# A hybrid two-block transformer on one core: in the recurrent stage the chunk inverse is kept as 64x64 blocks and turned on two quadrants, masked products alternate heads, one scan serves all chunks

## The chip, the cores and the metric

The kernel runs on one core of a Trainium2 chip. A core has TensorE (matmuls, PE in the rows; its weight loads are PEld), VectorE (DVE), ScalarE (ACT), GpSimd (POOL) and SyncE (SP, which issues the weight transfers). The metric is device time in microseconds for one launch, the median of several runs. Lower is better.

## The reference

Two transformer blocks with batch 1, 512 tokens and width 1024, in fp32. The first has sparse and latent attention and an MLP; the second, where the change lies, has an RWKV-7 mixer beside a convolution, a gated merge and an MLP. The mixer's recurrence, for each of 16 heads of 64 channels:

```
def _wkv7_scan(r, w, k, v, kk, a):
    """RWKV-7 recurrence. Inputs (B, T, H, N); state S (B, H, N_value, N_key).
    S_t = S_{t-1} diag(w_t) + (S_{t-1} (-kk_t)) (kk_t * a_t)^T + v_t k_t^T ;  o_t = S_t r_t
    """
    n_chunks = t // CHUNK
    ...
    _, o = lax.scan(chunk_step, S0, inputs)
```

CHUNK is 64, so there are 8 chunks. The kernel does not step through the tokens: within a chunk it builds a 64x64 triangular matrix from kk and a, inverts it by doubling blocks (5 levels), and then chains the 8 chunk states.

## The kernel before

The work is written out by hand, in one order for all engines. For the recurrent stage `rwkv_order()` yields a list of steps; each engine's program walks the same list and emits its own share of each step, with semaphores between the engines. An engine's instructions run strictly in this order. PSUM's banks are handed out in the list's order too (`begin` waits until the bank's former content has been emptied).

The stage is a loop over j = 0 to 7. A tile j is 128 channels, that is two heads (hh 0 and 1 on partitions 0 to 63 and 64 to 127); its 512 tokens stand as TT = 4 blocks t of 128, each two chunks. In quadrant form, the first chunk of a block is on rows 0 to 63, the second on rows 64 to 127 (`own_chunks`). A tile goes through these steps:

- `tok` turns four tiles to token-major form (L1139); `mb`, `mk` are the products of `arow` with `bh` and `kh` (L1147); VectorE masks them into `ma`, `mr`, `ka`, `kr` (L2142, L2144).
- `iy0` starts the inverse: head 0 on VectorE (L2132, L2133), head 1 on GpSimd (L738, L742). `ip` holds 64x64 blocks. `iy` (the inverse so far) and `ix` (its transpose) hold 128x128 per block t, of which only the chunks' own 64x64 blocks are read.
- `gnm`, `gnv`, `gnb`, `gnend`: the group norm of the tile before, put among these steps (L1239, L1243, L1125; VectorE L2189 and L2194 to L2204; ScalarE squares at L1625 and takes a root at L1628).
- for each level: `inv` turns `iy` on TensorE (L1156) and ScalarE copies it to `ix` (L1334); `ip` multiplies by `ma` (L1167) and VectorE masks it (L2153); `iy` multiplies (L1172) and VectorE adds (L2161).
- `akv`, `opv` (L1162, L1195), `tav` (L1178), `rr` (L1184), `opa` (L1202), `pt`, `qq`, then the chain of states `st` (L1226, L2182, L2185) and `ost` (L1234).

Between the steps stand parts of the next tile's projections (L765 to L767: three fp32r matmuls of 512 columns for each of 8 parts), its own first steps (`lw2`, `scan`, `kk`, ...), and on VectorE the 31 taps of the convolution (L2005). The weights of the projections are split into a high and a low half by ScalarE (L1295) and GpSimd (L680).

`scan` sums the log decays within each chunk: eight scans of 64 columns (L2071).

Of the kernel before, what the change touches and what calls it, by code (L numbers as in the profile page):

```python
# [24 lines left out]
P = 128  # L25
# [125 lines left out]
def rwkv_order():  # L151
# [3 lines left out]
    for j in range(KT):  # L155
# [16 lines left out]
        out += [("akv", j, 0), ("akv", j, 1), ("inv", j, 1, 0), ("opv", j, 0), ("opv", j, 1)]  # L172
# [10 lines left out]
        out += [("tav", j, 0), ("tav", j, 1)] + slot(1) + [("rr", j, 0), ("rr", j, 1)] + slot(1)  # L183
        out += [("opa", j, 0), ("opa", j, 1)] + last[:1] + [("pt", j, 0), ("pt", j, 1)] + last[1:2] + [("qq", j, 0), ("qq", j, 1)]
# [215 lines left out]
def rwkv_constants():  # L400
# [5 lines left out]
    out = [own(i < t), same & (i <= t)]  # L406
# [9 lines left out]
CONSTS = {"rw": (1 + LEVELS + 1 + 1) * CH + 2 * P, "eye_ones": 2 * P + H // 2, "alibi": S, "cmpb": TT * NC, "causal": S, "rope": S}  # L416


def build_program(nc, io):
    x_in, vec_in, w_in, out = io["x"], io["vec"], io["w"], io["out"]  # L420
    ctx = ExitStack()
    with ctx:
# [72 lines left out]
        with ExitStack() as at:  # L495
# [30 lines left out]
            ix, iy, ip = both("ix", TT * P), both("iy", TT * P), both("ip", TT * CH)  # L526
            iy2 = [m.rearrange("p t (c n) -> p t c n", c=2) for m in iy]
# [15 lines left out]
        strict, incl = rw[:, 0:CH], rw[:, CH:CH + P]  # L543
        level = [rw[:, CH * (3 + lv):CH * (4 + lv)] for lv in range(LEVELS + 1)]
        own_eye = rw[:, CH * (4 + LEVELS):CH * (5 + LEVELS)]
        heads = rw[:, CH * (5 + LEVELS):CH * (5 + LEVELS) + P]
# [125 lines left out]
        def _(pool):  # L672
# [22 lines left out]
            for f in rwkv_order():  # L695
# [28 lines left out]
                elif kind == "re":  # L724
                    wait_emptied(pool, ("rkv", j, 0))
                    pool.wait_ge(exp_ready, 2 * j + 2)
                    if j:
                        wait_filled(pool, ("mk", j - 1, 1))
                        wait_emptied(pool, ("rr", j - 1, 1))
                        wait_emptied(pool, ("rr", j - 1, 0))  # L730
# [3 lines left out]
                elif kind == "iy0" and f[2] == 1:  # L734
                    wait_emptied(pool, ("mb", j, 1))
                    if j:
# [5 lines left out]
                    pool.tensor_tensor(iy2[1], ip[1].unsqueeze(2).to_broadcast([P, TT, 2, CH]),  # L742
                                       own_eye.unsqueeze(1).unsqueeze(1).to_broadcast([P, TT, 2, CH]), ALU.add).then_inc(iy0_done[1], 1)
# [4 lines left out]
        def _(pe):  # L748
# [330 lines left out]
            for f in rwkv_order():  # L1079
# [69 lines left out]
                elif kind == "inv":  # L1149
# [5 lines left out]
                    for t in range(TT):  # L1155
                        mm = pe.transpose(b[:, t * P:t * P + P], iy[hh][:, t, :], eye)  # L1156
# [6 lines left out]
                elif kind == "ip":  # L1163
                    hh, lv = f[2], f[3]
                    wait_emptied(pe, ("inv", j, hh, lv - 1))
                    for t, own in own_chunks:
                        mm = pe.matmul(b[own, t * CH:t * CH + CH], ma[hh][own, t, :], ix[hh][own, t, own], start=True, stop=True)  # L1167
# [516 lines left out]
        def _(dve):  # L1684
# [330 lines left out]
            for f in rwkv_order():  # L2015
# [49 lines left out]
                elif kind == "scan":  # L2065
# [310 lines left out]
```

## Time and profile before

| | |
|---|---|
| median of 3 runs | 2250.59 us (2247.04 to 2252.44) |
| profiled execution | 2251.5 us, its span 2249.7 us |
| granted clock of TensorE, mean | 0.971 of 2.4 GHz |
| busy: TensorE, its weight loads | 2103.1 us, 1650.2 us |
| busy: VectorE, ScalarE, GpSimd | 1188.6 us, 800.9 us, 736.3 us |
| recurrent stage | about 1008 to 1648 us |

In a row of the profile, "L1184 PE MATMUL psum<-mr,tav 128*64 128x128" is an operation of line 1184 on TensorE that writes `psum` from `mr` and `tav`, with weights of 128 rows by 64 columns and an operand of 128x128. Matmul records overlap: the time that a block holds TensorE is read from its start to the next block's start. A plain fp32 matmul leaves two records, a transpose one. PEclk is the granted clock as a share of 2.4 GHz.

### The profile page before, as it was taken

Reading aid. Unit: us, or ns where it says so; the run is one execution under the profiler, and the core shown is the slowest. Engines: PE = TensorE matmul, PEld = TensorE weight load, DVE = VectorE, ACT = ScalarE, POOL = GpSimd, SP = SyncE. Lnnn points to the kernel's source line nnn. Section 1 sums busy time; section 2 is a strip of 40 time slices with the busy share of each in tenths; the row PEclk is TensorE's granted clock in tenths of the full one; section 3 lists DMA queues with packets and bytes.
Section 4 is the critical chain, followed back from the end, with each engine's and each line's share of the span. In section 5 each row is a group of like instructions: output and inputs, shape, how many; then the busy total and the mean of one; then the engine's idle time right before and its main releaser. Section 6 shows DMA issues by size and latency. Waiting matters only on the chain. (4 is left out here: it accounts for less than half of the span.)

```text
span 2249.7 us, 34219 instructions
## 1 busy us (share of the span) xinstructions
PE 2103.1 (93%) x13936; PEld 1650.2 (73%) x13936; DVE 1188.6 (53%) x1963; ACT 800.9 (36%) x1292; POOL 736.3 (33%) x347
## 2 busy tenths in 40 slices
PE   6898989999999999988999999999999998999997
PEld 5775567887788888766777776676777787888885
DVE  6427775333652342738778668777813456523322
ACT  2336655223332232443333333333333434322321
POOL 0221021444344444542232133223223443444442
PEclk9989999999899999999999999999999999999998
DMA  7531011533232333231101111101122322233331
GB/s 263 187 128 38 30 47 66 175 116 95 70 98 94 94 96 97 82 106 41 34 32 46 34 34 45 43 29 44 44 85 98 122 94 76 93 94 98 99 95 57
DMA packets 51450, 186.51 MB, mean 83 GB/s; under 512 B 5728, under 2 KB 6880, under 8 KB 50784
## 3 DMA queue, kind: packets, MB, share of 16 engines
q1 hardware_dynamic: 47520, 174.49, 23.8%
q10 hardware_dynamic: 3776, 9.83, 1.2%
q8 instruction: 113, 1.85, 0.4%
q14 instruction: 41, 0.34, 0.0%
HBM read 178.01 MB, written 6.29 MB: 82 GB/s over the span
## 5 line engine op out<-in xcount | busy, mean ns | idle before, releaser
L680 POOL TENSOR_TENSOR wlo<-raw,whi 128x1024 fp32r<-128x1024 f32 x266 | 644.5, 2424 | 1337.8 <-ACT whi L1295 1337.7
L765 PE MATMUL psum<-ah,whi 128*128 128x512 f32 x1288 | 538.2, 418 | 26.5 <-POOL wlo L680 16.0
L766 PE MATMUL psum<-ah,whi 128*128 128x512 f32 x1288 | 512.0, 398 | 0.0
L767 PE MATMUL psum<-ah,wlo 128*128 128x512 f32 x1288 | 511.6, 397 | 0.0
L1295 ACT ACTIVATE whi<-raw 128x1024 fp32r<-128x1024 f32 x266 | 280.2, 1054 | 367.2 <-PE psum L767 304.0
L765 PEld LDWEIGHTS psum<-ah,whi 128*128 128x128 f32 x1288 | 247.5, 192 | 98.2 <-POOL wlo L680 26.1
L767 PEld LDWEIGHTS psum<-ah,wlo 128*128 128x128 f32 x1288 | 247.2, 192 | 54.3
L766 PEld LDWEIGHTS psum<-ah,whi 128*128 128x128 f32 x1288 | 248.3, 193 | 43.5 <-issue 0.2
L2005 DVE SCALAR_TENSOR_TENSOR x<-upad,vec,x 128x512 f32<-128x512 f32 x240 | 211.5, 881 | 5.2
L765 PE MATMUL psum<-hidden,whi 128*128 128x512 f32 x536 | 213.0, 397 | 0.0
L766 PE MATMUL psum<-hidden,whi 128*128 128x512 f32 x536 | 212.7, 397 | 0.0
L767 PE MATMUL psum<-hidden,wlo 128*128 128x512 f32 x536 | 212.6, 397 | 0.0
L1716 DVE SCALAR_TENSOR_TENSOR hidden<-tmp,hidden 128x512 fp32r<-128x512 f32 x72 | 154.0, 2139 | 49.0 <-ACT hidden L1330 49.0
L765 PEld LDWEIGHTS psum<-hidden,whi 128*128 128x128 f32 x536 | 101.3, 189 | 24.5
L767 PEld LDWEIGHTS psum<-hidden,wlo 128*128 128x128 f32 x536 | 101.2, 189 | 24.5
L766 PEld LDWEIGHTS psum<-hidden,whi 128*128 128x128 f32 x536 | 101.2, 189 | 24.4
L1334 ACT ACTIVATE sq<-psum 128x512 f32<-128x512 f32 (+2 forms) x88 | 49.1, 572 | 195.9 <-PE psum L767 195.2
L1942 DVE TENSOR_TENSOR tmp<-sq 128x512 f32<-128x512 f32 x64 | 48.6, 759 | 105.6 <-ACT sq L1334 102.2
L1950 DVE TENSOR_TENSOR x<-psum,x 128x512 f32<-128x512 f32 x32 | 22.1, 692 | 142.2 <-PE psum L767 142.2
L1952 DVE SCALAR_TENSOR_TENSOR x<-psum,mod,x 128x512 f32<-128x512 f32 x32 | 24.0, 749 | 116.4 <-PE psum L767 116.3
L1334 ACT ACTIVATE ix<-psum 128x512 f32<-128x512 f32 x80 | 45.9, 597 | 75.4 <-PE psum L1156 74.6
L1427 ACT ACTIVATE sm<-sm,stat 128x128 f32<-128x128 f32 (+3 forms) x96 | 53.2, 555 | 42.4 <-DVE stat L1857 42.0
(340 smaller groups left out, 2916.8 us busy)
## 6 DMA issues: line engine op xcount, KB each, us to landing
raw<-in_w SPq DMA_DIRECT2D x322, 512.0 KB, 3.5
x<-in_x SPq DMA_DIRECT2D x1, 2048.0 KB, 7.9
x_kept<-x ACTq DMA_DIRECT2D x1, 2048.0 KB, 9.7
ao_kept<-ao ACTq DMA_DIRECT2D x8, 256.0 KB, 2.0
aof<-ao_kept ACTq DMA_DIRECT2D x1, 2048.0 KB, 10.8
x<-x_kept ACTq DMA_DIRECT2D x1, 2048.0 KB, 8.4
out<-x SPq DMA_DIRECT2D x1, 2048.0 KB, 6.3
lwt<-in_lw ACTq DMA_DIRECT2D x8, 128.0 KB, 2.0
```

Source lines behind the costliest of these rows:

```text
L680: pool.tensor_tensor(wlo[:, s % NHL, :], raw_of(SPLITS[s]), whi[:, s % NHL, :].bitcast(F32), ALU.subtract).then_inc(lo_done, 1)
L765: pe.matmul(dst, wh, h_, start=first, stop=False)
L766: pe.matmul(dst, wh, l_, start=False, stop=False)
L767: return pe.matmul(dst, wl, h_, start=False, stop=last)
L1295: act.activation(whi[:, s % NHL, :], raw_of(SPLITS[s]), ACT.Copy).then_inc(hi_done, 1)
L1334: emptied_by(act.activation(dst, bank(name) if src is None else src, kw.pop("func", ACT.Copy), **kw), name)
L1427: act.activation(probs[:, u % PROBS[tag], 0:w], probs[:, u % PROBS[tag], 0:w], ACT.Exp, bias=st[:, u % PROBS[tag], 0:1], scale=-1.0, accum ...
L1716: dve.scalar_tensor_tensor(dst_lo, tmp[:, n % NTMP, :], bias, dst_hi.bitcast(F32), ALU.add, ALU.subtract).then_inc(hl_ready, 1)
L1942: dve.tensor_tensor(slot(("hid", n, c, m)), sq[:, e % 2, :], sq[:, e % 2, :], ALU.mult).then_inc(pre_split, 1)
L1950: emptied_by(dve.tensor_tensor(x[:, m, :], bank(what), x[:, m, :], ALU.add), what)
L1952: emptied_by(dve.scalar_tensor_tensor(x[:, m, :], bank(what), gate(m), x[:, m, :], ALU.mult, ALU.add), what)
L2005: ins = dve.scalar_tensor_tensor(acc, src, tap, acc, ALU.mult, ALU.add)
```

## The change

Five edits, all in the recurrent stage:

1. `ix` and `iy` keep only the chunks' own blocks (64 columns per block t instead of 128). `inv` turns 64x64 blocks: chunk 0 of each block by a transpose in quadrant (0, 0), chunk 1 by a plain matmul with the identity in quadrant (64, 64), in turns. ScalarE's copy, VectorE's sum and both `iy0` steps halve their columns.
2. `opv`, `rr` and `opa` become one step each for both heads, with the heads alternating for each block t. They write the same places. `rr` needs one bank instead of two, and VectorE empties it with one operation of 128 rows instead of two of 64.
3. The four masked products into `mr` or `kr` become one of 512 columns.
4. The eight scans become one of 512 columns, which a constant `later` (0 at a chunk's first token, else 1) sets back at each chunk.
5. The constants `rw` grow by 512 columns for `later`.

```
-        out += [("tav", j, 0), ("tav", j, 1)] + slot(1) + [("rr", j, 0), ("rr", j, 1)] + slot(1)
-        out += [("opa", j, 0), ("opa", j, 1)] + last[:1] + [("pt", j, 0), ("pt", j, 1)] + ...
+        out += [("tav", j, 0), ("tav", j, 1)] + slot(1) + [("rr", j)] + slot(1)
+        out += [("opa", j)] + last[:1] + [("pt", j, 0), ("pt", j, 1)] + ...
...
-            ix, iy, ip = both("ix", TT * P), both("iy", TT * P), both("ip", TT * CH)
+            ix, iy, ip = both("ix", TT * CH), both("iy", TT * CH), both("ip", TT * CH)
...
                 elif kind == "inv":
-                    for t in range(TT):
-                        mm = pe.transpose(b[:, t * P:t * P + P], iy[hh][:, t, :], eye)
+                    for t, own in own_chunks:
+                        dst, src = b[own, t * CH:t * CH + CH], iy[hh][own, t, :]
+                        mm = pe.matmul(dst, src, eye[own, own], start=True, stop=True) if own.start else pe.transpose(dst, src, eye[own, own])
...
                 elif kind == "rr":
-                    wait_emptied(pe, ("tav", j, hh))
+                    for hh in range(2):
+                        wait_emptied(pe, ("tav", j, hh))
                     for t in range(TT):
-                        mm = pe.matmul(b[RN * hh:RN * hh + RN, t * P:t * P + P], tav[:, t, 0, hh, :], mr[hh][:, t, :],
-                                       start=True, stop=True)
+                        for hh in range(2):
+                            mm = pe.matmul(b[RN * hh:RN * hh + RN, t * P:t * P + P], tav[:, t, 0, hh, :], mr[hh][:, t, :],
+                                           start=True, stop=True)
...
-                    for c in range(NCK):
-                        cols = slice(c * CH, c * CH + CH)
-                        last = dve.tensor_tensor_scan(cw[:, cols], ones[:, 0:CH], sw[:, cols], 0.0, ALU.mult, ALU.add)
+                    last = dve.tensor_tensor_scan(cw[:, :], later, sw[:, :], 0.0, ALU.mult, ALU.add)
...
-                    for t in range(TT):
-                        last = dve.tensor_tensor(both_chunks[f[2]][:, t, :].rearrange("p (c n) -> p c n", c=2),
-                                                 full[:, t, CH:P].unsqueeze(1).to_broadcast([P, 2, CH]),
-                                                 incl.rearrange("p (c n) -> p c n", c=2), ALU.mult)
+                    emptied_by(dve.tensor_tensor(both_chunks[f[2]].rearrange("p t (c n) -> p t c n", c=2),
+                                                 full[:, :, CH:P].unsqueeze(2).to_broadcast([P, TT, 2, CH]),
+                                                 incl.rearrange("p (c n) -> p c n", c=2).unsqueeze(1).to_broadcast([P, TT, 2, CH]), ALU.mult), f)
...
-                    emptied_by(dve.tensor_tensor(iy2[f[2]], bank(f)[:, 0:TT * CH].rearrange("p (t n) -> p t n", t=TT)
-                                                 .unsqueeze(2).to_broadcast([P, TT, 2, CH]), iy2[f[2]], ALU.add), f)
+                    emptied_by(dve.tensor_tensor(iy[f[2]], bank(f)[:, 0:TT * CH].rearrange("p (t n) -> p t n", t=TT), iy[f[2]], ALU.add), f)
```

`opv` and `opa` are changed as `rr` is. Lines of the changed kernel have moved a little, so its rows carry its own numbers.

TensorE at the head of a tile j > 0, before. The rows are in program order; `x8` counts matmuls of the program.

```order
L1147 MATMUL psum<-arow,kh 64x128 x16
L1156 MATMUL psum<-eye_ones,iy 128x128 x4
L1243 MATMUL psum<-rw,sq 128x2 x4
L1162 MATMUL psum<-vtk,ka 64x64 x16
L1156 MATMUL psum<-eye_ones,iy 128x128 x4
L1195 MATMUL psum<-kr,vtk 64x128 x8
L1167 MATMUL psum<-ix,ma 64x64 x16
```

The same place in the changed kernel.

```order
L1145 MATMUL psum<-arow,kh 64x128 x16
L1155 MATMUL psum<-eye_ones,iy 64x64 x8
L1244 MATMUL psum<-rw,sq 128x2 x4
L1161 MATMUL psum<-vtk,ka 64x64 x16
L1155 MATMUL psum<-eye_ones,iy 64x64 x8
L1196 MATMUL psum<-kr,vtk 64x128 x8
L1166 MATMUL psum<-ix,ma 64x64 x16
```

Nothing changes its place. Each `inv` has eight operations of 64x64 for four of 128x128 (and sixteen for eight at levels 1 to 4, where both heads' stand together); the product of `kr` and `vtk` has the same eight matmuls, whose heads now alternate, which the rows don't tell.

VectorE at the head of a tile j > 0, before, from the masks of `mb` to the group norm's first step.

```order
L2142 TENSOR_TENSOR ma<-psum,rw 128x256
L2144 TENSOR_TENSOR mr<-psum,rw 128x128 x4
L2142 TENSOR_TENSOR ma<-psum,rw 128x256
L2144 TENSOR_TENSOR mr<-psum,rw 128x128 x4
L2132 TENSOR_TENSOR ip<-ma,rw 128x256
L2133 TENSOR_TENSOR iy<-ip,rw 128x512
L2189 SCALAR_TENSOR_TENSOR tmp<-psum,tmp 128x512
```

The same place in the changed kernel.

```order
L2137 TENSOR_TENSOR ma<-psum,rw 128x256
L2138 TENSOR_TENSOR mr<-psum,rw 128x512
L2137 TENSOR_TENSOR ma<-psum,rw 128x256
L2138 TENSOR_TENSOR mr<-psum,rw 128x512
L2128 TENSOR_TENSOR ip<-ma,rw 128x256
L2129 TENSOR_TENSOR iy<-ip,rw 128x256
L2176 SCALAR_TENSOR_TENSOR tmp<-psum,tmp 128x512
```

One product stands for four, and `iy` has half the columns; the order of the steps is as before.

## Rows read from the trace of the kernel before

**Rows 1.** TensorE in order of time, first steps of tiles 2, 3 and 4 (start, duration in us).

```profile
1251.22 0.66 PE L1139 MATMUL psum<-eye_ones,arow 128*128 128x128 f32 x4
...
1333.29 0.66 PE L1139 MATMUL psum<-eye_ones,arow 128*128 128x128 f32 x4
...
1413.85 0.66 PE L1139 MATMUL psum<-eye_ones,arow 128*128 128x128 f32 x4
```

**Rows 2.** Stretches: length, busy PE, PEld, DVE, ACT, POOL, clock, DMA share, GB/s.

```profile
1260.00:1265.00 5.00, 5.00 (x63) 4.37 (x65) 0.45 (x3) 3.67 (x6) 0.30 (x1) 0.66 0.01 3
...
1333.00:1414.00 81.00, 76.03 (x893) 57.19 (x888) 61.20 (x118) 29.32 (x45) 22.73 (x13) 1.00 0.12 39
```

**Rows 3.** TensorE's waits in 1060 to 1650 us: total, times, longest.

```profile
PE psum L1172 <- DVE ip L2153: 17.1, 13, 1.6
PE psum L1156 <- DVE iy L2161: 7.6, 13, 1.1
PE psum L1243 <- ACT ktok L1334: 3.4, 7, 0.5
```

**Rows 4.** TensorE in tile 3: two blocks of one form, and what follows each.

```profile
1346.35 1.09 PE L1125 MATMUL psum<-eye_ones,gnt 128*64 128x128 f32 x16
1347.37 0.50 PE L765 MATMUL psum<-ah,whi 128*128 128x512 f32 x1
...
1396.09 1.58 PE L1184 MATMUL psum<-mr,tav 128*64 128x128 f32 x16
1397.60 0.50 PE L765 MATMUL psum<-ah,whi 128*128 128x512 f32 x1
```

**Rows 5.** TensorE in tile 3: levels 2 to 4 of the inverse.

```profile
1360.47 0.40 PE L767 MATMUL psum<-ah,wlo 128*128 128x512 f32 x1
1360.70 1.04 PE L1156 MATMUL psum<-eye_ones,iy 128*128 128x128 f32 x8
1361.49 0.48 PE L765 MATMUL psum<-ah,whi 128*128 128x512 f32 x1
...
1362.72 0.39 PE L767 MATMUL psum<-ah,wlo 128*128 128x512 f32 x1
1363.04 1.15 PE L1167 MATMUL psum<-ix,ma 64*64 64x64 f32 x32
1364.12 0.50 PE L765 MATMUL psum<-ah,whi 128*128 128x512 f32 x1
...
1380.81 1.22 PE L1156 MATMUL psum<-eye_ones,iy 128*128 128x128 f32 x8 [1.08 <-DVE iy L2161]
```

**Rows 6.** VectorE's operations by form: busy us, mean ns; for scan and product: min/median/max.

```profile
L2161 DVE TENSOR_TENSOR iy<-psum,iy 128x512 f32<-128x512 f32 x72 | 46.3, 685 | 9.1 <-PE psum L1172 8.1
L2153 DVE TENSOR_TENSOR ip<-psum,rw 128x256 f32<-128x256 f32 x72 | 28.2, 420 | 25.5 <-PE psum L1167 24.2 <-DVE x L2005 0.2
...
L2071 DVE TENSOR_TENSOR_SCAN cw<-eye_ones,sw x64: 256/259/1697, 977.5 to 1526.2; 128x64 f32<-128x64 f32 x64
...
L2144 DVE TENSOR_TENSOR mr<-psum,rw x64: 277/279/282, 1010.3 to 1579.3; 128x128 f32<-128x128 f32 x64
```

**Rows 7.** VectorE in order of time: start of the stage, then tile 3.

```profile
940.68 0.18 DVE L2013 TENSOR_SCALAR omu<-vec 128x24 f32<-128x24 f32 x1 [3.45 <-DMA rw<-in_rw]
...
977.47 1.57 DVE L2071 TENSOR_TENSOR_SCAN cw<-eye_ones,sw 128x64 f32<-128x64 f32 x8 [7.37 <-ACT sw L1334]
...
1336.97 0.87 DVE L2144 TENSOR_TENSOR mr<-psum,rw 128x128 f32<-128x128 f32 x4
...
1338.20 1.10 DVE L2133 TENSOR_TENSOR iy<-ip,rw 128x512 f32<-128x512 f32 x1
...
1362.35 2.96 DVE L2071 TENSOR_TENSOR_SCAN cw<-eye_ones,sw 128x64 f32<-128x64 f32 x8
```

**Rows 8.** GpSimd in order of time, tile 3.

```profile
1337.92 0.84 POOL L738 TENSOR_TENSOR ip<-ma,rw 128x256 f32<-128x256 f32 x1 [12.72 <-DVE mr L2144]
...
1361.29 2.60 POOL L680 TENSOR_TENSOR wlo<-raw,whi 128x1024 fp32r<-128x1024 f32 x1 [13.33 <-ACT whi L1295]
```

More of the change, by code:

```diff
@@ L171, in rwkv_order @@
             out.append(("gnv", j - 1))
-        out += [("akv", j, 0), ("akv", j, 1), ("inv", j, 1, 0), ("opv", j, 0), ("opv", j, 1)]
+        out += [("akv", j, 0), ("akv", j, 1), ("inv", j, 1, 0), ("opv", j)]
         for lv in range(1, LEVELS + 1):
@@ L182, in rwkv_order @@
                 out += [("inv", j, 0, lv), ("inv", j, 1, lv)] + slot(2)
[L183 to L184 removed]
+        out += [("tav", j, 0), ("tav", j, 1)] + slot(1) + [("rr", j)] + slot(1)
+        out += [("opa", j)] + last[:1] + [("pt", j, 0), ("pt", j, 1)] + last[1:2] + [("qq", j, 0), ("qq", j, 1)]
         out += ahead + ([("re", j + 1)] if j + 1 < KT else [])
@@ L405, in rwkv_constants @@
     own = lambda m: np.where(i < CH, m[:, :CH], m[:, CH:])
-    out = [own(i < t), same & (i <= t)]
+    out = [own(i < t), same & (i <= t), np.broadcast_to(np.arange(S) % CH > 0, (P, S))]
     for lv in range(LEVELS + 1):
@@ L542, in build_program @@
         usig, og, tf = tmp[:, 0, :], tmp[:, 1, :], tmp[:, 2, :]
[L543 to L546, printed above, removed]
+        strict, incl, later = rw[:, 0:CH], rw[:, CH:CH + P], rw[:, CH + P:CH + P + S]
+        rest = rw[:, CH + P + S:]
+        level = [rest[:, CH * lv:CH * (lv + 1)] for lv in range(LEVELS + 1)]
+        own_eye = rest[:, CH * (1 + LEVELS):CH * (2 + LEVELS)]
+        heads = rest[:, CH * (2 + LEVELS):CH * (2 + LEVELS) + P]
         with ExitStack() as at:
@@ L1166, in _ @@
                     for t, own in own_chunks:
-                        mm = pe.matmul(b[own, t * CH:t * CH + CH], ma[hh][own, t, :], ix[hh][own, t, own], start=True, stop=True)
+                        mm = pe.matmul(b[own, t * CH:t * CH + CH], ma[hh][own, t, :], ix[hh][own, t, :], start=True, stop=True)
                 elif kind == "iy":
@@ L1171, in _ @@
                     for t, own in own_chunks:
-                        mm = pe.matmul(b[own, t * CH:t * CH + CH], ip[hh][own, t, :], iy[hh][own, t, own], start=True, stop=True)
+                        mm = pe.matmul(b[own, t * CH:t * CH + CH], ip[hh][own, t, :], iy[hh][own, t, :], start=True, stop=True)
                 elif kind == "tav":
@@ L2169, in _ @@
                         dve.wait_ge(ost_done, j)
-                    emptied_by(dve.tensor_tensor(rp[rows, :].rearrange("p (t n) -> p t n", t=TT),
-                                                 bank(f)[rows, :].rearrange("p (t n) -> p t n", t=TT), arow[rows, :, 1, :], ALU.add), f)
+                    emptied_by(dve.tensor_tensor(rp[:, :].rearrange("p (t n) -> p t n", t=TT), bank(f).rearrange("p (t n) -> p t n", t=TT),
+                                                 arow[:, :, 1, :], ALU.add), f)
                 elif kind == "pt":
```

49 lines of the change are left out of this document (18 added, 31 removed).

## The prediction

> **What bounds the kernel now.** I read the granted clock and busy shares by stretch first, then who waited for whom, then one tile of the recurrent stage in order of time on each engine. The recurrent stage is a fixed pattern: tile 3 begins at 1333.29 with the turn of `arow` and tile 4 at 1413.85, so a tile takes 80.56 us [rows 1]. In that tile TensorE shows 76.03 us of 81 busy, VectorE 61.20, ScalarE 29.32, GpSimd 22.73, all at full clock [rows 2]. The path through a tile is therefore TensorE's own queue, in its written order, broken by a few waits. Over tiles 1 to 7 (1060 to 1650 us) the three that the change can touch are, in total: 17.1 us for the level masks `ip` of VectorE, 7.6 us for its sums `iy`, 3.4 us for ScalarE's copy of `ktok` at the tile's head [rows 3]. So an edit pays in full only if it shortens a TensorE block, and otherwise only as far as one of these waits ends earlier.
>
> **The change part by part.**
>
> *Alternating heads (opv, rr, opa), three blocks per tile.* Each is 8 matmuls of 128 rows by 64 columns with 128 moving columns. Today four for head 0 (one half of the array's columns) come before four for head 1. The rr block runs from 1396.09 to the next block's start at 1397.60: 1.51 us for 16 records. The spread of `gnt` (L1125) has the same form, but alternates the halves: 1346.35 to 1347.37, 1.02 us for 16 [rows 4]. Alternation then saves 0.49 us a block; opv and opa are written alike, so 3 x 0.49 = 1.47 us a tile, **-11.8 us** for 8 tiles, on the path since the blocks stand in TensorE's queue.
> The row is at odds with a rule: the Trainium skill (TensorE: Matmul & The Clock Gate, Part 3, The mechanism) says that a weight load overlaps running matmuls only when the row group differs, and here only the column group does. By that rule this term would be 0 and the sum about -1 us. The rule is a rival below, and I follow the measured row.
>
> *Turning the inverse on two quadrants.* A pair of turns (both heads) today is 8 full transposes, one record each: it starts 0.23 us after the L767 before it (1360.47 to 1360.70) and the next block starts 0.79 us later (1361.49) [rows 5]. Afterwards it is 8 transposes of 64x64 in quadrant 0 (one record each, by the one-record transposes today) and 8 plain fp32 matmuls in quadrant 1 (two records each: L1167 shows 32 records for 16 matmuls), 24 records. The nearest row is L1167, 64x64 on the same two quadrants: 32 records in 1.08 us (1363.04 to 1364.12), entered 0.32 us after the L767 before it (1362.72) instead of 0.23 [rows 5]. Bounds for a pair: below, 24/32 of 1.08 is 0.81, plus 0.09 for entering, against 0.79, so +0.11; above, quadrant 1 with its two records a step sets the pace and the block takes all of 1.08, so +0.38. I take +0.33, nearer the upper end, since quadrant 1 alone has to do 16 records in a row. There are four such pairs in a tile (levels 1 to 4). The one at level 2 stands ahead of the long wait at level 3 and vanishes in it; three count: +1.0 us a tile, **+8 us**. The two single turns at the head stand beside 64x64 blocks already; I cost them at 0 (bounds -0.1 and +0.2 a tile).
>
> *Half-size work on ScalarE, VectorE, GpSimd.* The copy `ix` goes from 128x512 to 128x256, as does the `iy` sum: the sum takes 0.685 us now, a 128x256 one (`ip`) 0.420 [rows 6]. That is 0.26 us for the first head, and only the first head's is waited for at a block's start. `ix` lies ahead of L1167, which doesn't wait; nothing there. The four masked products of 128x128 per head take 0.87 us together; one 128x512 should take the 0.68 of the `iy` sum: -0.19 [rows 6, 7]. What each is worth on the path:
> - Head of the tile: gnv (L1243) waits 3.4 / 7 = 0.49 us [rows 3] for the bank that ScalarE empties into `ktok`; ScalarE comes to it only after squaring `og`, and that waits for VectorE's L2189, which stands behind two masked products and `iy0`. `iy0` on VectorE starts at 1338.20 and takes 1.10 us at 128x512, held up by GpSimd's L738 until 1338.76 [rows 7, 8]. With one product for four (-0.19) and half the columns in `iy0` (about 0.27 less), L2189 comes some 0.43 us earlier. -0.43 in seven tiles and about -0.5 in tile 0, which waits on the same steps: **-3.5 us**.
> - Level 1: the turn waits for the first sum too; the 13 waits for `iy` make 7.6 us [rows 3], seven of them about 1.08 at level 4 [rows 5], and nothing much is left by this count for level 1. I take the sum's 0.26 as the upper bound, nothing as the lower, and -0.24, since the block starts right behind the sum.
> - Level 3: L1172 waits for VectorE's masks, 1.6 us at the longest [rows 3]. VectorE is late because of the eight scans: 2.96 us from 1362.35, though the same eight alone take 1.57 [rows 7]. GpSimd's split (L680) runs from 1361.29 to 1363.89 [rows 8] and the scans get going when it ends. Then they need 1.42 us. One scan of 512 lies between two paces. A scan of 64 takes 0.26 us [rows 6]; 448 more columns at the 1.0 ns of the `iy` and `ip` operations ((685 - 420) / 256) make 0.71 us. Or at the pace of the eight: their step is (1.57 - 0.26) / 7 = 0.187 us; the masked products' step is (0.87 - 0.28) / 3 = 0.197 for 128 columns, of which 0.13 are columns and 0.065 launch; so 64 scanned columns cost 0.187 - 0.065 = 0.12 us, and 448 more make 0.26 + 0.85 = 1.11. I take the slow end: -0.3 here (-0.7 at the fast end). The rest of this wait stays, since GpSimd's split starts when it did.
> - Level 4: the turn waits 1.08 us (1380.81) [rows 5] behind VectorE's `kk` steps and two taps, which don't change; the sum itself is 0.26 shorter: -0.24. Level 5's wait for `ip` stands behind two taps and ScalarE's root for `nrt`, whose sizes stay; nothing. The product with `ftok` (L1178) follows the last sum and can gain 0.26 at most; the spread of `nrt` lies between, so I take 0.09.
> Together -0.87 us a tile, in seven tiles: **-6.1 us**.
>
> *One rr evacuation of 128 rows for two of 64.* VectorE saves 0.7 us a tile in a stretch where it has slack; nothing. The constants grow by 512 columns (384 to 640 KB). VectorE waits 3.45 us for them today, at 940.68 [rows 7]; 256 KB more cost nothing if TensorE's work ahead hides them, and at most their share of that wait, 3.45 x 256/384 = 2.3 us. I take **+0.5**, since much of the wait is the transfer's start.
>
> *Sum:* -11.8 + 8 - 3.5 - 6.1 + 0.5 = -12.9 us. The profiled execution took 2251.5 us (span 2249.7) and becomes 2238.6; the median of the runs is 0.9 us below it, so 2237.7. I say **2238**. A measurement of this kernel tells a change from none at about 0.2%, 4.5 us.
>
> **Rivals.**
> 1. *A transpose and a plain matmul, one after the other, don't overlap (slower).* The new block changes kind at every step: 16 changes in a pair, five pairs' worth in each of 8 tiles, 640 in all. For it speaks that entering another form costs 0.09 us today; against it that today's transposes follow L767 after the usual 0.23 us, without any gap, and that the tile form stays 64x64 throughout [rows 5]. At 0.09 us a change it is +58 us: 2238 + 58 = 2296. It decides from 13/640 = 0.02 us a change. A rule speaks for it as well: the Trainium skill (TensorEngine Tiling (Array Packing), Restrictions) says that column tiling disables transpose mode for fp32 input on trn2. No row here shows a column-tiled transpose. 0.11.
> 2. *Alternating heads brings nothing*, as the rule on row groups has it: -12.9 + 11.8 = -1.1, 2249.5, no change. L1125 speaks against it. 0.05.
> 3. *The waits don't shrink*, since GpSimd and the taps set VectorE's pace: without the 6.1 and half of the 3.5 it is -5: 2246. 0.08.
> 4. *The clock.* In two heads of tiles the granted clock is 0.66 over 5 us (the row of one of them stands here), so 1.2 GHz for much of it; in the five others it stays at 2.4 GHz, as in tile 3 [rows 2]. In these two tiles a tile takes 1.5 us longer: one of them begins at 1251.22, and the next at 1333.29, 82.07 against 80.56 [rows 1]. The new head is thinner: less time in full 128x128 work. If all seven fall it is +7.5 us, 2246; if none does, -3 us, 2235. 0.10 for the worse end.
>
> **How the numbers follow.** The forecast has 0.66 and its own range: with +0.11 a pair (-5.3 us) and the fast scan (-2.8) it is 2230; with the upper bounds of all costs and no gain at level 1, 2245, or 2247 with all of the constants' load. Rivals 3 and 4 reach to 2246 and the no-change rival to 2249.5, so 2228 to 2250 leaves out the slower case and little besides. Faster by over 0.2%: the forecast, rivals 3 and 4 in part, 0.78. Within 0.2%: 0.11. Slower: 0.11.
>
> **What would show each step.** The blocks of `mr` and `kr` with `tav` and `vtk` at 1.02 us from start to next start, instead of 1.51. The pair of turns at 0.9 to 1.1 us instead of 0.79, with 8 single and 16 double records. gnv's wait for ScalarE near 0.1; the wait for `ip` at level 3 near 1.1 to 1.3; tiles at 78.5 to 79.5 us instead of 80.56. The forecast is wrong if the turns take 2 us or more, or if the tile's heads run at 1.2 GHz.

## The result, and the profile after

The changed kernel takes **2366.93 us** (median of 4 runs, 2363.12 to 2375.8), the kernel before 2248.82 us (4 runs, 2246.37 to 2252.44): ratio 1.053, 95% interval 1.049 to 1.057. It is 5% slower, where 2238 was forecast. The profiled execution took 2363.12 us, its span 2361.3, with a mean granted clock of 0.948 against 0.971.

First the recurrent stage in the large. TensorE in order of time (start, duration in us), the first steps of three tiles, against [rows 1]. Counted from 0 they are tiles 3, 4 and 5; the tile called 3 ahead of the prediction, from 1333.29, is tile 4 by this count.

```profile
1295.98 0.66 PE L1137 MATMUL psum<-eye_ones,arow 128*128 128x128 f32 x4
...
1391.64 0.66 PE L1137 MATMUL psum<-eye_ones,arow 128*128 128x128 f32 x4
...
1484.53 0.66 PE L1137 MATMUL psum<-eye_ones,arow 128*128 128x128 f32 x4
```

A tile takes 95.66 and 92.89 us instead of 80.56. (Lines above 2000 and below 1200 have moved by a few; L1155 is the turn of the inverse, L1166 `ip`, L1171 `iy`, L763 to L765 the three products of one weight piece.) Next, where the tile grew. TensorE in tile 4, in order of time:

```profile
1398.31 1.78 PE L1155 MATMUL psum<-eye_ones,iy 64*64 64x64 f32 x12
1400.02 1.05 PE L1244 MATMUL psum<-rw,sq 128*128 128x2 f32 x8
...
1412.34 0.40 PE L765 MATMUL psum<-ah,wlo 128*128 128x512 f32 x1
1412.67 3.49 PE L1155 MATMUL psum<-eye_ones,iy 64*64 64x64 f32 x24
1416.09 0.50 PE L763 MATMUL psum<-ah,whi 128*128 128x512 f32 x1
...
1417.12 0.63 PE L764 MATMUL psum<-ah,whi 128*128 128x512 f32 x1
...
1418.11 1.97 PE L1166 MATMUL psum<-ix,ma 64*64 64x64 f32 x32
```

The pair of turns has the 24 records that were forecast, but holds TensorE for 1416.09 - 1412.67 = **3.42 us** instead of 0.79 [rows 5]; a single turn at the head takes 1.71. The block starts without a wait, so all of it is the block's own. It is no single case: of the 32 pairs 17 take 3.42 us. Right behind the pair the same matmuls last longer: L764 0.63 us instead of 0.40, L1166 1.97 instead of 1.15. The granted clock says why, in stretches of the same tile and of the stage (columns as in [rows 2]):

```profile
1060.00:1740.00 680.00, 667.07 (x6899) 490.02 (x6898) 406.44 (x693) 196.85 (x312) 159.15 (x93) 0.92 0.11 33
1412.00:1416.00 4.00, 4.00 (x28) 2.58 (x26) 3.71 (x7) 0.38 (x1) 0.00 (x0) 1.00 0.02 4
1416.00:1419.00 3.00, 3.00 (x24) 2.11 (x25) 0.00 (x0) 0.38 (x1) 0.00 (x0) 0.68 0.00 0
```

This pair itself runs at 2.4 GHz; the clock falls to 1.2 GHz behind it for some microseconds, and is 0.92 over the stage. It falls at the tiles' heads too, behind the first single turn or during the second: in the tile before this one the granted clock is 0.50 from 1304.50 to 1307.50, and the second single turn takes 2.56 us there (1308.00 to 1310.56). All seven heads from tile 1 on have such a fall. And the heads' alternation worked:

```profile
1374.84 1.09 PE L1184 MATMUL psum<-mr,tav 128*64 128x128 f32 x16
1375.86 0.50 PE L763 MATMUL psum<-ah,whi 128*128 128x512 f32 x1
```

1.02 us from start to next start, as L1125 promised [rows 4]. The waits of TensorE over the seven tiles (1060 to 1740 us; total, times, longest), against [rows 3]:

```profile
PE psum L1155 <- DVE iy L2151: 4.8, 7, 1.0
PE psum L1171 <- DVE ip L2143: 4.0, 4, 1.1
```

The wait for `ktok` is gone. TensorE became so slow that the others are rarely late: 28.1 us of waits in the three lines of [rows 3] have become 8.8.

### The profile page after: what moved, and what is told of

The parts are those of the page before. It is cut to its first block and busy times, and to the rows that moved or that the text cites. A ratio compares the mean times of both kernels' runs of the same rounds, so it can differ in the third digit from the quotient of the medians.

```text
span 2361.3 us, 35331 instructions
## 1 busy us (share of the span) xinstructions
PE 2237.0 (95%) x14576; PEld 1735.5 (73%) x14576; DVE 1155.2 (49%) x1803; ACT 788.3 (33%) x1292; POOL 731.1 (31%) x347
## 5 line engine op out<-in xcount | busy, mean ns | idle before, releaser
L763 PE MATMUL psum<-ah,whi 128*128 128x512 f32 x1288 | 544.0, 422 | 28.6 <-POOL wlo L680 16.9
L764 PE MATMUL psum<-ah,whi 128*128 128x512 f32 x1288 | 516.3, 401 | 0.0
L765 PE MATMUL psum<-ah,wlo 128*128 128x512 f32 x1288 | 515.9, 401 | 0.0
L763 PEld LDWEIGHTS psum<-ah,whi 128*128 128x128 f32 x1288 | 249.1, 193 | 102.8 <-POOL wlo L680 27.1
L765 PEld LDWEIGHTS psum<-ah,wlo 128*128 128x128 f32 x1288 | 249.8, 194 | 55.9
L764 PEld LDWEIGHTS psum<-ah,whi 128*128 128x128 f32 x1288 | 250.9, 195 | 43.9 <-issue 0.2
L763 PE MATMUL psum<-hidden,whi 128*128 128x512 f32 x536 | 212.5, 396 | 0.0
L764 PE MATMUL psum<-hidden,whi 128*128 128x512 f32 x536 | 212.4, 396 | 0.0
L765 PE MATMUL psum<-hidden,wlo 128*128 128x512 f32 x536 | 212.3, 396 | 0.0
L1155 PE MATMUL psum<-eye_ones,iy 64*64 64x64 f32 x960 | 146.8, 250 | 4.8 <-DVE iy L2151 4.8
L1155 PEld LDWEIGHTS psum<-eye_ones,iy 64*64 64x64 f32 x960 | 97.2, 127 | 66.1 <-issue 23.7
L765 PEld LDWEIGHTS psum<-hidden,wlo 128*128 128x128 f32 x536 | 101.0, 189 | 24.4
L763 PEld LDWEIGHTS psum<-hidden,whi 128*128 128x128 f32 x536 | 101.0, 188 | 24.5
L764 PEld LDWEIGHTS psum<-hidden,whi 128*128 128x128 f32 x536 | 101.0, 188 | 24.4
L2143 DVE TENSOR_TENSOR ip<-psum,rw 128x256 f32<-128x256 f32 x80 | 32.9, 424 | 134.2 <-PE psum L1166 133.8
L1335 ACT ACTIVATE ix<-psum 128x256 f32<-128x256 f32 x80 | 30.7, 383 | 184.1 <-PE psum L1155 184.1
## 6 DMA issues: line engine op xcount, KB each, us to landing
aof<-ao_kept ACTq DMA_DIRECT2D x1, 2048.0 KB, 11.2
```

Of the source, the lines that this page charges most:

```text
L763: pe.matmul(dst, wh, h_, start=first, stop=False)
L764: pe.matmul(dst, wh, l_, start=False, stop=False)
L765: return pe.matmul(dst, wl, h_, start=False, stop=last)
L1155: mm = pe.matmul(dst, src, eye[own, own], start=True, stop=True) if own.start else pe.transpose(dst, src, eye[own, own])
L1335: emptied_by(act.activation(dst, bank(name) if src is None else src, kw.pop("func", ACT.Copy), **kw), name)
L2143: emptied_by(dve.tensor_tensor(ip[f[2]], bank(f)[:, 0:TT * CH].rearrange("p (t n) -> p t n", t=TT), level[f[3]].unsqueeze(1).to_broadcast( ...
```

## The experiments

The theory after this reading (A): TensorE pays about 0.15 us each time it goes from a transpose to a plain matmul or back, 16 times in a pair. Rivals: a 64x64 transpose is slow by itself (B); the 64x64 plain matmul against the identity is (C); the clock, or the heads, are the cause and not the effect (D).

### Fewer changes of kind, the same work

Plain matmuls on both quadrants (e1_plain):

```
-  mm = pe.matmul(dst, src, eye[own, own], ...) if own.start else pe.transpose(dst, src, eye[own, own])
+  mm = pe.matmul(dst, src, eye[own, own], start=True, stop=True)
```

> The changed kernel, but the inverse is turned by plain matmuls on both quadrants (the same result; no transpose is left in it). Theory A (a change between transpose and plain matmul costs about 0.15 us, 16 changes in a pair of turns): no change of kind is left, a pair falls from 3.42 us to the 1.08 us of the ip block, a single turn from 1.75 to about 0.55; 4 x 2.34 + 2 x 1.2 = 11.8 us a tile, 94 us in all, and the granted clock of the recurrent stage goes back from 0.91 to near 1.0, another 10 to 30 us: 2238 to 2262 us. Theory B (a transpose on 64 columns is slow by itself): the same, since no transpose is left. Theory C (the 64x64 plain matmul against the identity is the slow half): the pair stays at 3.4 us and the time near 2367. Theory D (the clock fell for another reason, the blocks are long because of it): the clock stays at 0.91 and the pair above 2 us.

The four transposes first, then the four plain ones (e2_grouped), and in groups of two (e4_twos):

```
-  for t, own in own_chunks:
+  for t, own in own_chunks[0::2] + own_chunks[1::2]:                              # e2_grouped
+  for t, own in [own_chunks[i] for i in (0, 2, 1, 3, 4, 6, 5, 7)]:                # e4_twos
```

> The changed kernel, but in each turn the four transposes of quadrant 0 come first and then the four plain matmuls of quadrant 1: 2 changes of kind per turn in place of 8, 4 per pair in place of 16. The work is the same. Theory A: pair 1.08 + 4 x 0.15 = 1.7 us, single 0.85; 4 x 1.7 + 2 x 0.9 = 8.7 us a tile less, some 70 us: about 2297, a little less with the clock. Theory B: the transposes cost what they cost in any order: pair 3.2 to 3.5 us, 2360 to 2370. Theory C: the same as B. Against both stands that grouping loses the overlap of the two quadrants, which can add at most the 0.5 us of a block that doesn't alternate.

> The changed kernel, but transposes and plain matmuls in groups of two: 4 changes of kind per turn, 8 per pair, between the changed kernel (16) and the grouped one (4). Theory A, in a straight line over the number of changes: pair 1.08 + 8 x 0.15 = 2.3 us, about 2320 us. Theories B and C: pair 3.2 to 3.5 us, 2360 to 2370.

Full turns kept, all else changed but the scan (e3_fullturn):

```
-  for t, own in own_chunks:                       (and iy, ix 512 columns wide again)
-      ... 64x64 turns ...
+  for t in range(TT):
+      mm = pe.transpose(b[:, t * P:t * P + P], iy[hh][:, t, :], eye)
```

> The change without its first part: the inverse stays in 128x128 chunks and is turned by full transposes as before; the heads alternate in opv, rr and opa, the masked products are one each, rr is evacuated at once. The scan stays eight (its mask does not fit into the memory beside the wide inverse). By the terms of the prediction: -11.8 us for the heads, and -0.19 us of masked products per head at the tile's head, up to -2: 2235 to 2240. If the alternating heads brought nothing (the rule on row groups), 2247 to 2251. If the clock's fall were due to the alternating heads and not to the turns, the clock of the stage would be 0.91 here as well and the time above 2260.

| kernel | changes of kind in a pair | pair, us | median, us | ratio to before (interval) |
|---|---|---|---|---|
| changed | 16 | 3.42 | 2366.93 | 1.053 (1.049 to 1.057) |
| e4_twos | 8 | 2.40 | 2295.26 | 1.018 (1.016 to 1.021) |
| e2_grouped | 4 | 1.89 | 2267.43 | 1.007 (1.005 to 1.009) |
| e1_plain | 0 | 1.08 | 2228.6 | 0.989 (0.987 to 0.991) |
| e3_fullturn | full transposes | 0.79 | 2234.7 | 0.992 (0.990 to 0.994) |

(All 32 pairs of e1_plain take 1.08 us, and 18 of the 32 of e4_twos 2.40. In e3_fullturn 9 take 0.79, one of them from 1354.45 to 1355.24; 15 take 0.98 and 7 take 0.85.)

The pairs are read from rows like these, of e4_twos, e2_grouped and e1_plain, TensorE in order of time:

```profile
1364.64 2.47 PE L1155 MATMUL psum<-eye_ones,iy 64*64 64x64 f32 x24
1367.04 0.51 PE L763 MATMUL psum<-ah,whi 128*128 128x512 f32 x1
```

```profile
1360.40 1.96 PE L1155 MATMUL psum<-eye_ones,iy 64*64 64x64 f32 x24
1362.29 0.50 PE L763 MATMUL psum<-ah,whi 128*128 128x512 f32 x1
```

```profile
1360.46 1.15 PE L1155 MATMUL psum<-eye_ones,iy 64*64 64x64 f32 x32
1361.54 0.50 PE L763 MATMUL psum<-ah,whi 128*128 128x512 f32 x1
```

16, 8 and 4 changes lie on one line: (3.42 - 2.40)/8 and (2.40 - 1.89)/4 are both **0.1275 us a change**, over a base of 1.38; without transposes it is 1.08, the same as the `ip` block of that form [rows 5]. The starts of the single records say what the base is: within a group of e2_grouped a transpose follows another after 0.056 us, and the records of the plain matmuls of quadrant 1 follow each other after 0.058; 8 x 0.056 + 16 x 0.058 = 1.38. In e1_plain the records of the two quadrants start in twos, 0.007 us apart, every 0.058 us. So the other 0.30 us are the lost overlap of the quadrants. The times came out lower than theory A expected in all three: 2228.6 for 2238 to 2262, 2267.43 for 2297, 2295.26 for 2320; the price per change is 0.1275 and not 0.15, and what the clock gives back was a guess. B and C fall: the same operations in another order cost 1.5 us less, and the plain matmuls alone are the fastest of the quadrant turns. D falls too: the long pair itself ran at a granted clock of 1.00, and with the heads alternating the stage's clock is 1.00 in e1_plain and e3_fullturn.

### Is it the kind?

A by itself is too simple, and the next four show it.

```
e5_fewer:      only chunks 0 and 2 of quadrant 0 by transpose, order as in the change
e6_same:       the same, but quadrant 0 whole (T P T P), then quadrant 1 (P P P P)
e7_fullmix:    e3_fullturn with  pe.matmul(dst, src, eye) if t % 2 else pe.transpose(dst, src, eye)
e8_fullplain:  e3_fullturn with  pe.matmul(dst, src, eye)  alone
```

> The changed kernel, with half as many transposes: in quadrant 0 only chunks 0 and 2 are turned by a transpose, 1 and 3 by a plain matmul; the order of the quadrants is that of the changed kernel (transpose, plain, plain, plain, and again). 8 transposes in a pair of turns in place of... 4, and 8 changes of kind in place of 16, as many changes as the kernel in groups of two. Theory A (so much per change; the three blocks measured so far, 3.42 us at 16 changes, 2.40 at 8, 1.89 at 4, lie on 1.38 + 0.1275 n): 2.40 us, or down to 2.1 if the plain ones between them overlap again (1.08 + 8 x 0.1275). Theory B' (the cost is that of a transpose on a column tile, less when it follows another one): 4 transposes, each alone, (3.42 - 1.08) / 8 = 0.29 each: 1.08 + 4 x 0.29 = 2.25. The time by A: 2280 to 2295.

(The changed kernel has 8 transposes in a pair; this one has 4.)

> As the kernel with fewer transposes, but quadrant 0 first (transpose, plain, transpose, plain) and then four plain matmuls on quadrant 1: again 8 changes of kind in a pair, now all inside one quadrant. If the change of kind costs by itself (A): 2.3 to 2.5 us, as for the groups of two, 2295. If it costs only where the two kinds stand on different quadrants (C2: the two quadrants can't run in different modes at the same time, while one quadrant may change at will): no change crosses a quadrant but the entry, and the pair takes 1.4 to 1.7 us, the time is near 2255.

> The kernel that keeps the full 128x128 turns (2234.7 us), with chunks 1 and 3 turned by a plain 128x128 matmul against the identity and 0 and 2 by a transpose as before: 8 changes of kind in a pair, on the whole array and not in quadrants. If the price of a change is general: halfway between 0.79 us and the pair of the kernel with plain matmuls alone (its control, in the same call, about 1.1 to 1.7 us), and 6 changes x 0.1275 = 0.8 more; with a plain pair of 1.3 us that is 1.8 us. If it is a matter of column tiles only: the halfway value, about 1.0 us.

> Control for the last one: the kernel with the full 128x128 turns, all done by plain matmuls against the identity. No change of kind. 16 records of 128 columns: by the blocks of mr with tav (16 records, 1.02 us alternating halves, 1.51 not) between 1.0 and 1.7 us a pair in place of 0.79; 3 to 4 pairs a tile on the path, 8 tiles: 5 to 25 us more than 2234.7 us.

Measured: e5_fewer a pair of 2.18 us (1368.72 to 1370.90) and 2285.0 us; e6_same 2.43 (1371.78 to 1374.21) and 2295.14; both have 8 changes. For e5_fewer the base without lost overlap gives 1.08 + 8 x 0.1275 = 2.10. Half the transposes at as many changes bring 0.22 us or nothing, and the quadrants need not alternate for the price to be there. But e7_fullmix and e8_fullplain, TensorE in order of time:

```profile
1360.02 1.49 PE L1157 MATMUL psum<-eye_ones,iy 128*128 128x128 f32 x12
1361.27 0.48 PE L765 MATMUL psum<-ah,whi 128*128 128x512 f32 x1
```

```profile
1360.13 1.95 PE L1156 MATMUL psum<-eye_ones,iy 128*128 128x128 f32 x16
1361.83 0.48 PE L765 MATMUL psum<-ah,whi 128*128 128x512 f32 x1
```

Full transposes alone take 0.79, full plain ones 1.70, the mixture 1.25: just the mean, with 8 changes of kind in it. **On the whole array a change of kind costs nothing** (2247.07 us, between 2234.7 and 2256.85). Theory A as put is wrong; the price belongs to part tiles.

### Is it the tile?

Theory F: what costs is a change of the array's form, and the 64x64 transpose has another form than the 64x64 matmul. Its rival, theory K: what costs is a change of kind on a part tile. Three kernels add a 64x64 step of quadrant 0 ahead of each full turn, which then overwrites it with the same values; the fourth doubles the grouped transposes.

```
e11_tile_plain: + pe.matmul(*quarter, start=True, stop=True)   ahead of each full plain turn
e12_tile_turn:  + pe.transpose(*quarter)                       ahead of each full plain turn
e13_turn_turn:  + pe.transpose(*quarter)                       ahead of each full transpose
e14_doubled:      for t, own in own_chunks[0::2] * 2 + own_chunks[1::2]:
```

> The kernel with full 128x128 turns by plain matmuls (pair 1.70 us), with one more plain matmul of the 64x64 block of quadrant 0 ahead of each (its result is overwritten with the same values). 16 changes between a 64x64 tile and the whole array in a pair, none of kind. Theory F (what costs is a change of the array's form, and a transpose counts as another form than the 64x64 tile): 1.70 + 8 x 0.07 + 16 x 0.13 = 4.3 us. Theory K (what costs is a change of kind on a 64x64 tile): 1.70 + 0.56 = 2.3 us, plus at most 0.09 a change to the tile, 3.0.

> The same, with the added 64x64 matmul replaced by a 64x64 transpose of the same block: 16 changes of kind and of tile in a pair. Theory F with the transpose on the whole array's form: no change of form, 1.70 + 8 x 0.07 = 2.3 us. Theory K: 2.3 + 16 x 0.13 = 4.4 us.

> The kernel with full 128x128 transposes (pair 0.79 us), with a 64x64 transpose of the block of quadrant 0 ahead of each. Only the size of the tile changes, 16 times in a pair, the kind never. Theory F, if a 64x64 transpose is not of the whole array's form: 0.79 + 0.56 + 16 x 0.13 = 3.4 us. Theory K: 0.79 + 0.56 = 1.35 us.

> The kernel with grouped turns (pair 1.89 us, 4 changes of kind), with the four transposes of quadrant 0 made twice in each turn before the four plain matmuls of quadrant 1: 8 transposes more in a pair, no further change. If a 64x64 transpose behind another one is cheap, as the full ones are (0.79 us for 8, some 0.07 to 0.1 each): 2.45 to 2.7 us. If each waits for the one before it: 8 x 0.2 or more, 3.5 us and above.

The pairs (and the times, one run each: 2418.15, 2387.88, 2349.96, 2282.12 us): e11_tile_plain 5.21 us (1350.22 to 1355.43), e12_tile_turn 4.57 (1336.80 to 1341.37), e13_turn_turn 3.29 (1419.73 to 1423.02), e14_doubled 2.33 (1368.89 to 1371.22). e11 has no transpose at all, and pays more than any; theory K had 2.3 to 3.0 us for it and theory F 4.3, so F is nearer and still 0.9 short. e13 has nothing but transposes and pays (3.29 - 0.79 - 0.44)/16 = 0.129 us for each change of size, where K had none. e14 adds 8 transposes and only 0.44 us, 0.055 each: a 64x64 transpose is cheap behind another one. So form and not kind, as F has it. e12 alone comes out near K's figure (4.4), but F had 2.3 for it only if a 64x64 transpose were of the whole array's form, and by e13 it isn't. Single steps of e11_tile_plain, e12_tile_turn and e13_turn_turn:

```profile
1350.22 0.32 PE L1157 MATMUL psum<-eye_ones,iy 64*64 64x64 f32 x2
1350.47 0.49 PE L1158 MATMUL psum<-eye_ones,iy 128*128 128x128 f32 x2
```

```profile
1336.80 0.24 PE L1157 MATMUL psum<-eye_ones,iy 64*64 64x64 f32 x1
1336.97 0.49 PE L1158 MATMUL psum<-eye_ones,iy 128*128 128x128 f32 x2
```

```profile
1419.73 0.24 PE L1157 MATMUL psum<-eye_ones,iy 64*64 64x64 f32 x1
1419.90 0.33 PE L1158 MATMUL psum<-eye_ones,iy 128*128 128x128 f32 x1
```

Leaving a 64x64 plain matmul takes 0.25 us, leaving a 64x64 transpose 0.17, whatever of another form comes next. The two together are 0.43 with the rows' rounding, and a step of the changed kernel's turns is 3.42/8 = 0.4275: its transposes and matmuls treat each other like operations of another form. Which form the transpose has, a row of the changed kernel suggested, at level 3:

```profile
1343.03 0.69 PE L1113 MATMUL psum<-lh,lwt 64*128 64x512 f32 x1
1343.04 0.24 PE L1155 MATMUL psum<-eye_ones,iy 64*64 64x64 f32 x1
1343.57 0.59 PE L1113 MATMUL psum<-lh,lwt 64*128 64x512 f32 x1
1344.09 3.32 PE L1155 MATMUL psum<-eye_ones,iy 64*64 64x64 f32 x23
```

The first transpose starts 0.01 us after a matmul of 64 rows by 128 columns that runs for 0.69 us, while the plain matmul after it starts only at 1344.09, when both are all but through. Theory R: the transpose runs as a tile of 64 rows by all columns. Last pair, with four steps ahead of each full plain turn:

```
+  pe.transpose(turned, block, eye[0:CH, 0:CH])
+  pe.matmul(b[:, t * P:t * P + CH], iy[hh][0:CH, t, :], eye[0:CH, 0:CH], ...)   # e15_rows: 64 rows, 128 columns
+  pe.matmul(turned, block, eye[0:CH, 0:CH], ...)                                # e16_quads: 64 by 64
```

> The kernel with full turns by plain matmuls (pair 1.70 us), with four steps more ahead of each turn: a 64x64 transpose of a block of quadrant 0, then a plain matmul that contracts the same 64 rows but fills all 128 columns (its results are overwritten with the same values). In the traces so far a 64x64 transpose starts beside a running 64-row, 128-column matmul, while a 64x64 plain one waits for it. Theory R (a 64x64 transpose runs as a tile of 64 rows by 128 columns; what costs is only a change between that tile, the 64x64 one and the whole array): 16 changes of kind but none of form between the added steps, about 0.06 + 0.135 us each pair of steps: 1.70 + 8 x 0.2 + 4 changes of form x 0.13 = 3.7 us. Theory K (the change of kind on a part of the array costs): 1.70 + 8 x 0.43 + 0.3 = 5.4 us.

> The control: the same with the added plain matmul on the 64x64 quadrant, as in the changed kernel but in the same quadrant as the transpose. Both theories: 8 x 0.43 + 1.70 + 0.3 = 5.4 us, the step from transpose to plain matmul 0.175 and back 0.25 us, as in the changed kernel.

e15_rows, then e16_quads, in order of time:

```profile
1339.22 0.24 PE L1157 MATMUL psum<-eye_ones,iy 64*64 64x64 f32 x1
1339.30 0.38 PE L1158 MATMUL psum<-eye_ones,iy 64*128 64x64 f32 x2
1339.52 0.22 PE L1157 MATMUL psum<-eye_ones,iy 64*64 64x64 f32 x1
```

```profile
1363.84 0.24 PE L1157 MATMUL psum<-eye_ones,iy 64*64 64x64 f32 x1
1364.01 0.33 PE L1158 MATMUL psum<-eye_ones,iy 64*64 64x64 f32 x2
1364.26 0.24 PE L1157 MATMUL psum<-eye_ones,iy 64*64 64x64 f32 x1
```

Next to the matmul of twice the columns the transpose lets go after 0.06 us (0.08 for the first), next to the small one after 0.17. The four pairs of steps take 1.23 us (1339.22 to 1340.45) against 1.70 (1363.84 to 1365.54); in time 2364.15 against 2427.91 us, one run each. The step back, 0.22 us, is more than the 0.135 expected, but it holds no price. The matmul has two records; in the trace the second starts 0.112 us after the first, and the transpose 0.112 us after the second (1339.300, 1339.412, 1339.523), and the records of the full plain matmuls alone follow each other after 0.112 us as well. The transpose in turn lets go after 0.056 us, as behind another transpose. So alternating the two costs nothing here. A whole pair takes 4.47 us in e15_rows (1325.51 to 1329.98), where R had 3.7 and K 5.4; 1.70 + 8 x 0.28 + 4 x 0.13 gives it, with the matmul at what it takes. In e16_quads it takes 5.42 (1361.03 to 1366.45), where both had 5.4. In the same kernel as the first, e15_rows, four transposes and four such matmuls all start while L1115 (64 rows, 128 columns) is running:

```profile
1336.89 0.69 PE L1115 MATMUL psum<-lh,lwt 64*128 64x512 f32 x1
1336.89 0.24 PE L1157 MATMUL psum<-eye_ones,iy 64*64 64x64 f32 x1
...
1337.42 0.59 PE L1115 MATMUL psum<-lh,lwt 64*128 64x512 f32 x1
...
1337.81 0.38 PE L1158 MATMUL psum<-eye_ones,iy 64*128 64x64 f32 x2
1338.13 1.16 PE L1160 MATMUL psum<-eye_ones,iy 128*128 128x128 f32 x8
```

R holds. The Trainium skill (TensorEngine Tiling (Array Packing), Tiling Modes, Key Properties) says that changing the tiling mode, not just the tile, drains TensorE. The rows agree with it, and with the restriction of the Trainium skill that the prediction named, that column tiling and the fp32 transpose exclude each other: next to a 64-column matmul the transpose lets go after 0.17 us, next to a 128-column one after 0.06, and every step of the new turn is a change of mode.

### The other parts, in the kernel with plain turns

```
e9_halves:       for hh in range(2):  for t in range(TT):     (opv, rr, opa: head 0, then head 1)
e10_manysmall:   eight scans of 64, four masked products of 128x128 per head, as before the change;
                 the constants without `later`
```

> The kernel with plain turns (2228.6 us), with the alternation of heads in opv, rr and opa undone: four matmuls of head 0, then four of head 1, in one block. By the term of the prediction, 0.49 us a block, 3 blocks, 8 tiles: 11.8 us more, 2240.4. If the weight load never overlapped across column groups (the rule on row groups), no difference: 2228 to 2230.

> The kernel with plain turns, with VectorE's small part undone: eight scans of 64 in place of one of 512, four masked products of 128x128 per head in place of one. By the terms of the prediction: 0.19 us at the tile's head and 0.3 us at level 3, 4 us in all, less 0.5 for the constants: 2232. If the split of GpSimd holds VectorE either way: only the head's 0.19 in 8 tiles, 2230. If none of it is on the path: 2228.6.

> The kernel with plain turns once more, for these two to be compared with on the same chip: 2228.6 us, ratio 0.989.

e9_halves: 2243.29 us (0.9965, 0.9951 to 0.9978) against 2228.63 (0.9898, 0.9882 to 0.9913) for e1_again on the same chip: **14.7 us** for the alternation of heads, 11.8 expected. Its block:

```profile
1392.04 1.58 PE L1184 MATMUL psum<-mr,tav 128*64 128x128 f32 x16
1393.55 0.50 PE L763 MATMUL psum<-ah,whi 128*128 128x512 f32 x1
```

1.51 us against 1.03 in e1_again (1384.20 to 1385.23). The rest, 3 us, has no line of its own; the medians' spread is of that size.

e10_manysmall: 2228.46 us, no difference from e1_again. TensorE's waits in it, then in e1_again:

```profile
PE psum L1171 <- DVE ip L2153: 13.3, 13, 1.1
PE psum L1244 <- ACT ktok L1335: 2.4, 7, 0.4
```

```profile
PE psum L1171 <- DVE ip L2143: 11.2, 13, 1.1
PE psum L1244 <- ACT ktok L1335: 1.1, 7, 0.2
```

These waits are 3.4 us longer with the small operations (3.1 with the one for `iy`, which goes from 4.3 to 4.0), as the terms had it, while the medians say nothing of it. The intervals reach some 4 us to either side, so this stays inconclusive: worth 0 to 4 us.

## Why the prediction was wrong

- **The step that failed** is the overlap in "Turning the inverse on two quadrants": the bounds of a pair, +0.11 and +0.38 us, are those of L1167, plain matmuls on both quadrants, and let transposes and plain matmuls run side by side. What should have warned of it is in rival 1, which had 0.11; against it stood "that the tile form stays 64x64 throughout". It does for the operands as the rows print them, 64*64, and not for the array. The term, +0.33 us a pair, was +2.63 (3.42 - 0.79); a single turn, costed at nothing, went from 0.59 (in e3_fullturn, 1416.34 to 1416.93) to 1.71. With 24 records for the pair and each kind's pace right, no count of records could have shown it.
- The rival's own price was short as well. It took 0.09 us from the entry into L1167; where the changes follow each other one costs 0.1275 (that the 0.09 is the same thing, partly hidden, is likely and not shown). 640 changes make 82 us, not 58. The alternating quadrants also no longer overlap, 1.38 - 1.08 = 0.30 a pair.
- **From the plain turns to the changed kernel**, the span grows from 2227.1 (e1_again) to 2361.3: 134.2 us. The blocks make 8 x (4 x 2.34 + 2 x (1.71 - 0.56)) = 93.3. The waits shrink from 16.6 to 8.8, -7.8. That leaves 48.7 us, which is a remainder and not measured by itself; of what the rows show, the clock is what is left that moved. For 1060 to 1630 us, in the changed kernel and in e1_again:

```profile
1060.00:1630.00 570.00, 558.79 (x5763) 409.14 (x5762) 339.96 (x582) 167.96 (x266) 132.35 (x79) 0.92 0.11 33
```

```profile
1060.00:1630.00 570.00, 546.35 (x7311) 413.12 (x7311) 404.85 (x700) 194.11 (x312) 157.21 (x92) 1.00 0.13 40
```

  0.08 of the stage's 763 us is 61 us at the most, so the remainder has room in it. The clock is not a cause of its own: with 16, 8, 4 and 0 changes it is 0.92, 0.95, 0.98 and 1.00 in this stretch. Nor are the transposes needed for its fall: e11_tile_plain, which has none, stands at 0.93 in the same stretch. What rival 4 named came true, the clock fell in all seven heads, but with the single turns there: in e1_again, whose heads have as little full-size work, it falls in none of the seven. It fell behind pairs as well, and by the remainder it cost some 49 us where rival 4 had 7.5.
- **The heads' alternation** (-11.8) was right in mechanism and slightly small: block 1.51 to 1.02 us, 14.7 us by e9_halves. Rival 2 falls. The rule on row groups (the Trainium skill, TensorE: Matmul & The Clock Gate, Part 3, The mechanism), by which this term would be 0, does not give what these fp32 matmuls show: the row group is the same, only the column half alternates, and a block takes 0.48 us less.
- **The head's wait**: forecast 0.43 us less in each tile; it goes from 3.4 us to 1.1 in the kernel with plain turns, 0.33 a tile. Levels 1, 3 and 4: 17.1 + 7.6 to 11.2 + 4.3 us, 1.3 a tile where 0.87 was forecast (the longer pairs ahead of the waits may help; no run separates that). By the waits, rival 3 falls.
- **The one scan** was put at 1.11 us from the end of GpSimd's split, where the eight need 1.42. It takes 1.2 us alone and 2.81 in six of eight tiles, since the split runs beside it. VectorE's scan and GpSimd's split in a tile of the changed kernel:

```profile
1331.67 2.35 POOL L680 TENSOR_TENSOR wlo<-raw,whi 128x1024 fp32r<-128x1024 f32 x1 [17.25 <-ACT whi L1296]
1332.29 2.81 DVE L2070 TENSOR_TENSOR_SCAN cw<-rw,sw 128x512 f32<-128x512 f32 x1
```

  The split ends at 1334.02 and the scan at 1335.10, 1.08 us later: this term was right (-0.34 for -0.3), although the scan's whole duration beside the split, 2.81 for 2.96, hardly shows it.
- **The constants**: +0.5 was forecast; the wait for `rw` went from 3.45 to 4.25 us [rows 7], +0.8:

```profile
941.74 0.18 DVE L2014 TENSOR_SCALAR omu<-vec 128x24 f32<-128x24 f32 x1 [4.25 <-DMA rw<-in_rw]
```

- With the turns made plain, the change pays, and more than was forecast: 2228.6 us, 1.1% faster than before and level with e10_manysmall as the fastest here. It is 24.4 and 21.2 us under the kernel before (e1_plain and e1_again, each against the runs beside it), where all parts together had -12.9: -14.7 for the heads' alternation, -11.5 of waits (28.1 to 16.6), +5.9 for the pairs and +0.8 for the constants make -19.5. A pair then takes 1.08 us and is entered 0.33 us after the matmul before it instead of 0.23, together +0.39, the upper bound of the forecast (+0.38). It beats the full transposes (2234.7): the waits of the three lines are 26.9 us there and 16.6 here, 10.3 less, and its 32 pairs take 34.6 us against 28.7, 5.9 more. That leaves 4.4 of the 6.1 us; the rest is within the runs' spread.

## What to carry to other kernels

Before putting transposes and matmuls side by side on parts of TensorE's array, ask which tile the array takes for each, not which shape the row prints: an fp32 transpose of 64x64 runs as 64 rows by all columns, and each step between that, a 64x64 matmul and the whole array costs 0.13 to 0.16 us here. Turn small blocks by a plain matmul against the identity when their neighbours are small plain matmuls, or group by form; on the whole array the two kinds mix freely. A block with many such changes can cost a second time: here the clock fell to 1.2 GHz behind it, for about half as much again.

## What the runs showed of the hardware

- The price of a change of form, with nothing to wait for: 0.1275 us between 64x64 transposes and matmuls, in pairs and in single turns alike (8 changes and 1.71 us in the changed kernel's, 4 and 1.20 in those of e4_twos); 0.129 between transposes of two sizes; between the 64x64 transpose and the full plain matmul (4.57 - 1.70 - 0.44)/16 = 0.15; between 64x64 and full plain matmuls (5.21 - 1.70 - 8 x 0.117)/16 = 0.16. Between full transposes and full plain matmuls, and between 64x64 transposes and matmuls of 64 rows by 128 columns: none.
- A 64x64 fp32 transpose behind another one costs 0.055 us; a full one 0.1; a full plain matmul against the identity 0.21, two records 0.11 us apart; a 64x64 plain one 0.0675 when the quadrants alternate, 0.117 (two records, 0.058 each) in one quadrant.
- The profile's busy share does not show what the changes of form cost: TensorE stood at 667.07 of 680 us busy in the changed kernel against 554.34 of 590 (1060 to 1650 us) before, for the same seven tiles. The length of a block, from its start to the next block's start, shows it.
- The clock can fall behind such blocks while TensorE's row reads fully busy (1416 to 1419 us: 3.00 of 3.00 us, clock 0.68), with transposes in them or without (0.92 and, in e11_tile_plain, 0.93 over the same stretch).
